# First modulation by column halves, with the keys' and values' products begun on four of eight chunks

## What is computed

```
sh1, sc1, gt1, sh2, sc2, gt2 = modulation(c, w_mod, b_mod)     # silu(c) @ w_mod + b_mod, w_mod is 1024 x 6144
csh1, csc1, ...              = modulation(c_ctx, w_mod, b_mod)
hx = rms_norm(x, norm1_g) * (1.0 + sc1) + sh1
hc = rms_norm(ctx, norm1_g) * (1.0 + csc1) + csh1
qx, kx, vx, bx, cx, ux = in_proj(hx, w_in, q_norm_g, k_norm_g)  # h @ w_in, split by columns
qc, kc, vc, bc, cc, uc = in_proj(hc, w_in, q_norm_g, k_norm_g)  # only keys and values are used of the context
```

## Time and profile before

| what | value |
|---|---|
| median of three runs | 1496.44 us (1491.52 to 1498.91) |
| the profiled execution: its own time | 1496.4 us |
| the profiled execution: its span | 1494.3 us |
| PE busy | 1444.4 us, 97% of the span |
| DVE busy | 640.4 us, 43% |
| ACT busy | 452.6 us, 30% |
| chain that ended last, by engine | PE 73%, DMA 21%, DVE 3% |
| read from HBM | 479.20 MB |

### The profile page before, as it was taken

How to read it: one execution, slowest core, us unless ns; L and a number is a source line. 1 busy time by engine, 2 the same in 40 slices (tenths; PEclk the granted TensorE clock), 3 DMA queues, 4 the chain that set the end, 5 groups by cost and what they waited for, 6 DMA issues and landing times.

```text
span 1494.3 us, 23446 instructions
## 1 busy us (share of the span) xinstructions
PE 1444.4 (97%) x9948; PEld 1018.2 (68%) x9948; DVE 640.4 (43%) x1022; ACT 452.6 (30%) x686; POOL 27.2 (2%) x36
## 2 busy tenths in 40 slices
PE   6999999999999999999999999999999999999997
PEld 3976864444454444444444459999999778999997
DVE  5787430011110011001001029888878776655555
ACT  3435231111111111111111125443344354455453
POOL 0011000000000000000000000000020000000000
PEclk9999999999999999999999989999999999999999
DMA  9959989999999999999999995888767631456551
GB/s 359 355 208 347 366 344 431 426 433 426 429 433 429 427 426 431 429 428 431 431 425 433 427 390 201 310 309 309 246 212 282 261 113 31 154 169 198 195 168 56
DMA packets 117428, 481.01 MB, mean 322 GB/s; under 512 B 12109, under 2 KB 59466, under 8 KB 96770
## 3 DMA queue, kind: packets, MB, share of 16 engines
q1 hardware_dynamic: 115936, 476.46, 81.2%
q0 software_dynamic: 736, 2.31, 0.5%
q10 hardware_dynamic: 705, 1.51, 0.3%
HBM read 479.20 MB, written 1.06 MB: 321 GB/s over the span
## 4 chain that ended last, share of the span: by engine, by line
PE 73%; DMA 21%; DVE 3%; ACT 1%; issue 1%; SPq 0%; DVEq 0%; ACTq 0%
DMA arena<-in_w_up_dram 18%; PE psum L1682 15%; PE psum L1814 8%; PE psum L1880 7%; PE psum L1704 6%; PE psum L1792 6%; PE psum L1787 5%; PE psum L1800 3%; PE psum L1782 3%; PE psum L1392 3%; PE psum L1663 2%; PE psum L1645 2%; DMA arena<-in_w_in_dram 2%; PE psum L1573 2%; DMA arena<-in_ffn_w_in_dram 1%; PE psum L1268 1%
## 5 line engine op out<-in xcount | busy, mean ns | idle before, releaser
L1682 PE MATMUL psum<-arena,squares 128*64 128x384 f32 x2048 | 340.8, 490 | 19.0 <-DMA arena<-in_w_up_dram 10.6
L1682 PEld LDWEIGHTS psum<-arena,squares 128*64 128x64 f32 x2048 | 146.9, 138 | 214.9 <-issue 188.8
L2430 DVE TENSOR_TENSOR mixT<-mixT,psum 128x384 f32<-128x384 f32 x32 | 26.5, 827 | 495.1 <-PE psum L1682 495.1
L1704 PE MATMUL psum<-arena,small 128*64 128x512 f32 x768 | 171.9, 596 | 0.0
L1704 PEld LDWEIGHTS psum<-arena,small 128*64 128x64 f32 x768 | 52.3, 137 | 96.2 <-issue 94.4
L2499 DVE TENSOR_TENSOR ff_w_lo<-arena,ffn_w_hi 128x2048 fp32r<-128x2048 f32 x44 | 100.5, 2284 | 0.0
L1792 PE MATMUL psum<-ff_x_parts,ff_w_lo 128*128 128x256 f32 x704 | 91.5, 283 | 0.0
L1792 PEld LDWEIGHTS psum<-ff_x_parts,ff_w_lo 128*128 128x128 f32 x704 | 88.9, 192 | 1.6
L1074 ACT ACTIVATE ffn_w_hi<-arena 128x2048 fp32r<-128x2048 f32 x44 | 83.9, 1907 | 6.8 <-DMA arena<-in_ffn_w_in_dram 6.8
L1045 ACT ACTIVATE small<-psum 128x384 f32<-128x384 f32 x32 | 15.7, 490 | 212.4 <-PE psum L1690 212.4
L1787 PE MATMUL psum<-ff_x_parts,ffn_w_hi 128*128 128x512 f32 x336 | 79.9, 390 | 0.0
(11 more groups left out here) (373 smaller groups left out, 1975.0 us busy)
## 6 DMA issues: line engine op xcount, KB each, us to landing
arena<-in_w_gate_dram SPq DMA_DIRECT2D x32, 3072.0 KB, 32.2
arena<-in_w_up_dram SPq DMA_DIRECT2D x31, 3072.0 KB, 33.0
arena<-in_w_down_dram SPq DMA_DIRECT2D x31, 3072.0 KB, 31.9
arena<-in_ffn_w_in_dram SPq DMA_DIRECT2D x44, 1024.0 KB, 7.6
arena<-in_w_ada_dram SPq DMA_DIRECT2D x18, 2048.0 KB, 12.8
arena<-in_w_mod_dram SPq DMA_DIRECT2D x11, 2048.0 KB, 14.5
arena<-in_ffn_w_out_dram SPq DMA_DIRECT2D x22, 1024.0 KB, 4.9
arena<-in_w_in_dram SPq DMA_DIRECT2D x10, 2048.0 KB, 10.3
```

Source lines behind the costliest of these rows:

```text
L1682: last = pe.matmul(b[64 * half:64 * half + 64, 0:HALF_E], lhsT=xeT[:, k, u * SLOTS:(u + 1) * SLOTS], rhs=w[:, k, half * HALF_E:(half + 1) ...
L1704: last = pe.matmul(bank[6][64 * half:64 * half + 64, :], lhsT=hiddenT[:, f % 3, 64 * (f // 3):64 * (f // 3) + 64], rhs=down[:, f, half * 5 ...
```

## The change

**Loads.** The 2048 columns are split otherwise. `mod0` and `mod1` now hold the columns of chunks 0 to 3 (512 of the shift, 512 of the scale) for all 1024 rows, `mod2` and `mod3` those of chunks 4 to 7. Each piece is two DMAs in runs of 2 KB (the last piece four DMAs in two parts). The order is `mod0`, `mod1`, `w_kv`, `mod2`, `mod3`; the bytes are the same.

**Work.** The modulation is taken in two halves (banks 4 and 5, one turn to columns each). When the first half is there, chunks 0 to 3 of c1 and n1 are scaled, shifted and multiplied with the high and low weights of keys and values; the other four chunks follow after the second half. The products are the same in number, in another order. Four small DVE instructions, one PSUM copy, one turn (four products) and two products with zeros (which open banks 4 and 5) are added; of the 32 `keep_busy` products ahead of the keys and values 21 are left. The angles' DVE instructions move ahead of the norm's reciprocal, the copy of `bias_turn` behind the first scaling, and the load of more constants on ACT's queue stays behind the last piece.

```
@@ loads on SyncE
+            def load_mod(i, reader):
+                slot, _ = PLACE[("pre", f"mod{i}")]
+                half, first_k = i // 2, 4 * (i % 2)
+                parts = ((0, 4, f"ring_full{slot}"),) if i < N_MOD_PIECES - 1 else ((0, 2, f"ring_full{slot}"), (2, 4, "last_mod_full"))
+                for lo, hi, arrived in parts:
+                    for s in range(2):
+                        at = 1024 * s + 512 * half
+                        sp.dma_start(mod_w(i)[:, lo:hi, s, :], chunked(w_mod[P * (first_k + lo):P * (first_k + hi), :], at, at + 512))\
+                          .then_inc(sem(arrived), 16)
...
-            for name, reader in PRE:
+            for name in ["mod0", "mod1", "w_kv", "mod2", "mod3"] + [name for name, _ in PRE if name != "w_kv" and name[:3] != "mod"]:
@@ ACT
+            first_round("z_k")
+            first_round("z_v")
+            shift_half(0)
+            act.wait_ge(sem("pieces_read"), N_MOD_PIECES)
+            act.dma_start(consts[:, more_consts], ins["shape_constants"][:, more_consts]).then_inc(sem("more_consts_loaded"), 16)
+            act.wait_ge(sem("bias_stored"), 16)
+            shift_half(1)
@@ PE
+            mod_piece(0)
+            keep_busy(9, 7)
             pe.wait_ge(sem("token_rstd_ready"), 1)
...
+            mod_piece(1)
             b = open_job("bias_turn")
...
+            turn_half(bank[6], 1).then_inc(sem("late_turned"), 1)
             keep_busy(3, 7)
...
+            keys_values_hi(0)
+            mod_piece(2)
+            keys_values_lo(0)
+            mod_piece(3)
+            for key, x, at in (("c1", c1_lo, 0), ("n1", x1_lo, T)):
+                for b, w in ((b_k, k_hi), (b_v, v_hi)):
+                    rests(0, key, x, at, b, w)
+            close_job(turn_half(open_job("mod_turn"), 2))
+            keep_busy(3, 7)
+            open_job("z_k")
+            keys_values_hi(1)
+            keys_values_lo(1)
+            for b, w in ((b_k, k_hi), (b_v, v_hi)):
+                rests(1, "c1", c1_lo, 0, b, w)
+            close_job(rests(1, "n1", x1_lo, T, b_k, k_hi, True))
             open_job("z_v")
+            close_job(rests(1, "n1", x1_lo, T, b_v, v_hi, True))
@@ DVE
+            dve.wait_ge(sem("pieces_read"), 2)
             nc.vector.tensor_copy(mod_acc[:, 0, :], bank[4][:, :]).then_inc(sem("rows_copied"), 1)
+            dve.wait_ge(sem("late_turned"), 1)
+            take_half(0, bank[6], step)
+            b = take_job("bias_turn")
...
             first_rest("z_k")
             first_rest("z_v")
+            half_rests(0)
+            dve.wait_ge(sem("pieces_read"), N_MOD_PIECES)
+            nc.vector.tensor_copy(mod_acc[:, 0, :], bank[5][:, :]).then_inc(sem("rows_copied"), 1)
+            take_half(1, take_job("mod_turn"), mod_closed)
+            half_rests(1)
             first_rest("z_q0")
```

More of the change, by code:

```diff
@@ L147, in ring_places @@
             if name != "mla_up":
-                loads[s] += 3 if (part, name) in W_OUT else 8 if name == "w_q" else 1
+                loads[s] += 3 if (part, name) in W_OUT else 8 if name == "w_q" else 2 if name.startswith("mod") else 1
             place[(part, name)] = (s, loads[s])
@@ new lines, in keys_values_lo, with rests @@
+            def keys_values_lo(half):
+                for name, b, w in (("z_k", b_k, k_lo), ("z_v", b_v, v_lo)):
+                    pe.wait_ge(sem("mid_lo"), ROUNDED[name])
+                    for x, at in ((c1_hi, 0), (x1_hi, T)):
+                        for k in range(4 * half, 4 * half + 4):
+                            pe.matmul(b[:, at:at + T], lhsT=w[:, k], rhs=x[:, k, :], start=False, stop=False, skip_group_check=True)
+            def rests(half, key, x, at, b, w, closes=False):
+                for k in range(4 * half, 4 * half + 4):
+                    pe.wait_ge(sem("mix_x_lo"), half_place(key, k) + 1)
+                    last = pe.matmul(b[:, at:at + T], lhsT=w[:, k], rhs=x[:, k, :], start=False, stop=closes and k == KD - 1,
+                                     skip_group_check=True)
+                return last
@@ new lines, in _, with take_half, rows @@
+            for at, what in ((0, "x"), (T, "ctx")):
+                b = take_job(f"spread_{what}")
+                empty_job(nc.vector.tensor_copy(rstd[:, at:at + T], b[:, 0:T]))
+            def take_half(half, b, done):
+                own = slice(4 * half, 4 * half + 4)
+                def rows(dst, s):
+                    b_rows = b[:, 0:32].rearrange("p (m x h s) -> p s h x m", m=4, x=2, h=2)
+                    dst, cols = (ap[:, 0:16].rearrange("p (x h m) -> p h x m", x=2, h=2) for ap in (dst, cols_a))
+                    return nc.vector.tensor_tensor(dst[:, half], b_rows[:, s, half], cols[:, half], ALU.add)
+                rows(mod_ctx, 1)
+                done(rows(mod, 0))
+                for key, scale in (("c1", mod_ctx), ("n1", mod)):
+                    at = SET[key] * KD
+                    i = nc.vector.scalar_tensor_tensor(out=gains[:, at + own.start:at + own.stop],
+                                                       in0=scale[:, KD + own.start:KD + own.stop], scalar=1.0,
+                                                       in1=cols_a[:, 48 + own.start:48 + own.stop], op0=ALU.add, op1=ALU.mult)
+                step(i)
+                for key, src, dst, stat in (("c1", ctxT, mixT, rstd[:, T:2 * T]), ("n1", xT, hT, rstd[:, 0:T])):
+                    for k in range(own.start, own.stop):
+                        nc.vector.scalar_tensor_tensor(out=dst[:, k, :], in0=src[:, k, :], scalar=gain(key, k), in1=stat,
+                                                       op0=ALU.mult, op1=ALU.mult).then_inc(sem("norm_scaled"), 1)
```

161 lines of the change are left out of this document (69 added, 92 removed).

## The result

| what | before | after |
|---|---|---|
| median, runs side by side | 1496.07 us (1491.34 to 1499.25) | 1499.57 us (1493.26 to 1503.90) |
| ratio, 95% interval | | 1.0025 (1.0015 to 1.0034) |
| the profiled execution: its own time | 1496.4 us | 1495.6 us |
| the queries' first product (the marker) | 51.93 us | 56.10 us |
| first expert's first product | 206.98 us | 212.83 us |

By the ratio, the change makes the kernel slower by 3.7 us (2.2 to 5.1), where 1.1 us faster was forecast. The profiled execution of the changed kernel lies 4 us under its median, and the executions of one kernel spread over 8 to 11 us (the ranges in the table), so single spans say nothing here. The marker and the ratio carry the comparison.

What follows compares the result with a forecast made beforehand. The early chain was bound by the w_kv transfer, then PE; step sums put the queries' first product at 50.8 instead of 51.93 us, 1.1 us earlier: 1496.4 - 1.1 = 1495.3 us, range 1490.5 to 1500.

Steps and rivals of the forecast that it cites:

- The failed step: PE's modulation pieces: mod1 and mod2 were to take 1.85 us each, mod3's two parts 1.0 us each.
- Reciprocal finished: DVE's reciprocal of the norm, behind the ctx copies and angles, was to be done at 21.4 us, against 18.95 before.
- the spread: PE's spreading of the norms after the reciprocal was to take 1.1 us and end at 22.6.
- Eight scalings: DVE's scaling of the first half's chunks was to take 3.25 us, from 27.25 to 30.5.
- last scaling to the end of PE's products: In the first half, PE's chunk products were to end 1.24 us behind DVE's last scaling, at 31.75.
- The strided take of 32 columns: DVE's four new strided copies, two in each half, had no row and were taken as 0.18 us each.
- The last piece's wait: Last part of mod3 was to land at 36.1 and be multiplied at 37.8, without a DMA wait, 1.7 us margin.
- The shift reaches the end: A shift of the queries' first product was counted one for one in the kernel's time: 1.1 us earlier.
- The first: Rival: PE reaches mod3's last part sooner through a quicker first half; 1.7 us more gain, 1493.6 us; chance 0.14.
- The second: Rival: the modulation pieces land late because shorter runs cost more; far bound 1505.5 us; chance 0.05.
- The third: Rival: PE's clock falls through fewer fillers and more waits; likely 1497 to 1499 us, up to 1508; chance 0.07.
- The fourth: Rival: the shift is lost behind the queries' first product in a transfer not moving with PE; 1496.4 us; chance 0.10.

Runs made afterwards that it cites:

- e8: The changed kernel with eight filler products instead of three behind the second turn to columns; 1499.8 us in one run.
- e7: The changed kernel with piece products on all four output bands, the new selection tile allocated behind all other tiles; ratio to the kernel before 1.0003.
- e1: The changed kernel with piece products on all four output bands, its new 16-byte tile shifting later tiles; 1490.3 us, ratio to the kernel before 0.9968.
- e4: e1 with the second turn ahead of the latent rest products and two fillers instead of six in the last piece; 1489.9 us, ratio 0.9961.
- e3: The changed kernel with each piece's products grouped one band at a time, last piece unsplit, six fillers left out; 1504.1 us, ratio 1.0057.
- e2: The kernel before with the products of its first three pieces ordered by pairs of bands; 1495.4 us, ratio 0.9999.

## Why the prediction was wrong, step by step

**The failed step** is a duration: "multiplies `mod1` (1.85) to 24.45", then "`mod2` (1.85, landed)" and "first part (1.0)" and "last part (1.0)" of `mod3`. I took the duration from a row of the kernel before whose form (`128*32 128x512`) and count (x16) are those of the changed kernel. The form doesn't say to which band each product writes, and that is what the change alters. The price is 3.56 - 1.85 = 1.71 us for each piece. `mod1`, `mod2` and `mod3` are on the path: 5.1 us. `mod0` was counted as covered by the wait for the reciprocal, and it was: `mod1` began at 22.62, by the sum at 22.6. So 50.8 + 5.1 = 55.9, measured 56.10. The rest is a difference of small terms: the clock took 0.7 us (from e8), and from the end of a turn to the first scaling it was 0.6 us both times where the sum has 0.8. The runs show the price: with four bands and every tile in its place (e7) the marker is at 51.47, and from the reciprocal's end to it there are 29.3 us, by the sum 29.4. The time is that of the kernel before. The forecast of 0.1% under it lies in e7's interval, so the runs neither show nor refute that gain.

**Steps that held.**
- Reciprocal finished at 21.4 by the sum, 21.17 measured; the spread to 22.6, measured 22.68.
- Eight scalings in 3.25 us, measured 28.68 to 31.93; last scaling to the end of PE's products 1.24 us, measured 33.06 - 31.93 = 1.13.
- The strided take of 32 columns: 0.15 to 0.17 us each, taken as 0.18.
- The last piece's wait: none on the DMA. Two products at once made PE later still (41.89 instead of 37.8), so this says less than it seems. In e1 it came at 38.77 and in e4 at 37.32, without a DMA wait either; so the transfers had landed by 37.3.
- The shift reaches the end: the marker moved by 4.2 us, the time by 3.7 (2.2 to 5.1); in e3 by 10.9 and 8.5 (5.4 to 11.7).

**Rivals.** The first (PE sooner, 1493.6) needed a short first half and did not come. The second (late pieces) is refuted by the row at 41.89. The third (the clock) did come, in four of the seven profiles with this order of work, and more often than its chance of 0.07 says; but where the same rows stand with and without it, it cost 0.7 us (changed kernel against e8) and 1.0 us (e1's third piece, 2.88 instead of 1.92), not several. It may be why e7 isn't quicker than the kernel before with a marker 0.5 us earlier, which is not shown. Its 1497 to 1499 us lie near the measured time, but it would have been right for a wrong reason: e7 and e1, in whose profiles the clock fell too, show that the loss goes away with the bands. The fourth (a shift lost behind the marker) is refuted by e3. No rival named the products of the pieces. That an instruction of the same form keeps its duration was the premise of the whole sum, and no bound was put on it.

**The range.** The measured 1499.57 lies inside the range, near its upper end, but by luck: the width had been made for other causes. The chance of "slower" by over 0.5% was small, and it did not come, but the cost that did come had no part in that chance.

## What to carry to other kernels

When an edit regroups small matmuls, list for each group the output bands (or row groups) that are in use near each other, before and after; the same instructions took nearly twice as long here with half the bands (3.63 against 1.92 us). Splitting a block of columns over two bands by even and odd chunks of rows and adding them in the following product kept all four busy, and the turn behind them took the same time (1.05 us in e1, 1.06 in the changed kernel). When an experiment adds even a tiny tile, run a control with an unused tile of the same size: here it was worth 0.2 to 0.3%, as much as the effect under study.

## What the runs showed of the hardware that I had not expected

- Products of other bands are begun ahead of those that precede them in the program: e2's order by pairs still had four in flight in the first slot and 1.94 us per piece. With runs of four products on one band (e3) the look ahead reached only in part, and the piece took 5.37 us; the other band's first instruction began when three of the busy band's had still to begin.
- The distance in SBUF between a product's moving rows and its weights changes dense products by 1% (282 against 279 or 280 ns). Moving all tiles by 16 bytes doesn't (282 ns, ratio 0.9999), and products whose operands moved together kept their 283 ns.
- Weights in runs of 2 KB came at 386 GB/s in 15 to 20 us, and with `w_kv`'s runs of 1 KB among them at 366 in 20 to 25 us, against 421 in runs of 8 KB. The Trainium skill ("DMA: Bandwidth & Descriptors", section Specifications) puts the full rate at 512 B and above. The trace doesn't agree: the window with 2 KB runs is 8% below the longer runs.
